# A conv stage rearranged: projection begun during the token tiles, products and low halves on VectorE, 36 taps ahead of attention

## The chip, the cores and the metric

The kernel runs on one core of a Trainium2 chip. The metric is the device time of one execution in microseconds. The five engines that matter are TensorE (matmuls and transposes, PE in the profile), VectorE (DVE), ScalarE (ACT), GpSimd (POOL) and SyncE (SP), whose queue issues almost all transfers.

## What is computed

One step of a hybrid decoder layer over 1024 prompt tokens and 8 x 8 sample tokens, padded to nine tiles of 128 tokens. The part that the change touches is the conv group of the input projection:

```python
xn = rmsnorm(h, g_mix)
z = xn @ w_in
q, k, v, og, lr, cv = jnp.split(z, SPLITS, axis=-1)
...
a, gate = jnp.split(cv, 2, axis=-1)
u = a * jax.nn.sigmoid(gate)
c, buf_new = causal_depthwise_conv(u, buf0, w_conv, b_conv)   # 31 taps per channel
c = jax.nn.silu(layernorm(c, g_conv_ln, b_conv_ln))
h = h + jnp.concatenate([o, c], axis=-1) @ w_out
```

`o` is the output of four heads of gated linear attention, computed in chunks. A top-2 mixture of 32 experts, a gated embedding and a last norm follow. All weights are fp32 and the matmuls of the projections run as three fp16 passes: each operand is split into a high half (its rounding to fp16) and a low half (the rest).

## The kernel before

The program is written by hand for each engine; semaphores order the engines, and within an engine the text order is the order of execution. Line numbers in this document are those of the kernel before, unless a row of the changed kernel shows others.

1. *Norm and transposes (0 to 36 us).* SP loads nine x tiles with two in flight (`load_x`, L492). ScalarE squares and takes the root (`norm_x`, L859 and L864), VectorE scales the tile by the gain (`norm_x`, L1199; two SBUF inputs), TensorE transposes it in eight pieces (`transpose_x`, L1668), ScalarE writes the high half (`evac_xT`, L869) and VectorE the low half (`evac_xT`, L1205; one input in PSUM).
2. *Conv projection (36 to 134 us).* For each of four channel groups c, TensorE computes part 0 (the gate) and then part 1 (a) for three blocks of 384 tokens, 24 matmuls a block and part (L1683), so 144 a group. ScalarE makes the high half of the group's weights w_cv[c] (`split_cv`, L878), GpSimd the low half (L687). ScalarE evacuates the gate with a sigmoid into `sg_sb` and a with a copy into `a_sb` (L914). GpSimd multiplies them into `u` (L702, L703). Beside this the 16 pieces of the token weights w_tok come in through two raw buffers, `side0` and `side1`: SP loads one when the low half of the piece before it in that buffer is done (`load_wt`, L505), ScalarE makes the high half (`split_wt`, L901), GpSimd the low half (L692). VectorE runs the depthwise taps of c = 0 and 1 once a group's `u` is there: tap 0 is a scale and a bias (L1235), each other one a multiply and add over 1024 tokens (L1238), and each waits for the one before. `REST = 9` of the 31 taps of a channel group are left for later, so 44 taps stand here. VectorE's next instruction after them is `log_gate(0)` (L1259).
3. *Attention (134 to 367 us).* TensorE projects tile n + 1 (`z`, L1691; `z_lr`, `z_qk`, `z_v`, `z_og`) among the attention steps of tile n: `turn` (L1735 to L1739), `scores` (L1746), `cumulate` (L1723, L1727; it wants `la` of VectorE), `outputs` (L1757 to L1761). Between its attention steps VectorE runs the taps that are left, `BESIDE` = 10 a tile, in groups of 3, 3 and 4. In a tile it does `qT_out` (L1275), 3 taps, `mask_scores` (L1279), `log_gate` (L1259), 3 taps, `state` (L1286), `decay_qk` (L1264, L1265), 4 taps, `gate` (L1270). GpSimd scales the state (L716, L718) and runs the taps of the sample tokens (L729, L733).
4. *Output stage, experts and the rest (367 to 1123 us).* VectorE first makes the low halves of w_out (L1316), whose raw buffers SP refills in turn; then come the conv's layer norm, the output projection, the router, the experts (L1907 to L1938), the embeddings (L1989, L1999). The change touches only names of semaphores here.

The order of the change's surroundings is set by these queues and by what each part waits for:

```python
pl.wait_ge(cv_sb, 6 * (c + 1))       # GpSimd's product: both parts of all three blocks
dve.wait_ge(u_rdy, 2 * (c + 1))      # VectorE's first tap of a group
pe.wait_ge(cv_sb, 6 * CC)            # TensorE before z_lr(0)
pe.wait_ge(wt_lo, 2 * KC)
```

## Time and profile before

| | us |
|---|---|
| three runs, median (lowest, highest) | 1126.66 (1126.3, 1128.25) |
| the profiled execution, its own time | 1125.14 |
| its span, first to last instruction | 1123.3 |
| TensorE busy | 1008.9 (90%) |
| VectorE busy | 721.1 (64%) |
| ScalarE busy | 473.6 (42%) |
| GpSimd busy | 295.3 (26%) |
| mean granted clock of TensorE | 0.946 |

The span is what the rows' times count from; the profiled execution's own time is 1.84 us longer. Busy shares are over the whole span, and a stage can have another limit than the mean shows. A row of the order of time reads: start, duration, engine, line, operation, output and inputs with their shapes, how many instructions are merged, and in brackets how long the engine stood idle before it and what released it. The granted clock is a share of TensorE's full speed: 1.0 is 2.4 GHz, 0.5 is 1.2 GHz.

### The profile page before, as it was taken

Reading aid. Unit: us, or ns where it says so; the run is one execution under the profiler, and the core shown is the slowest. Engines: PE = TensorE matmul, PEld = TensorE weight load, DVE = VectorE, ACT = ScalarE, POOL = GpSimd, SP = SyncE. Lnnn points to the kernel's source line nnn. Section 1 sums busy time; section 2 is a strip of 40 time slices with the busy share of each in tenths; the row PEclk is TensorE's granted clock in tenths of the full one; section 3 lists DMA queues with packets and bytes.
Section 4 is the critical chain, followed back from the end, with each engine's and each line's share of the span. In section 5 each row is a group of like instructions: output and inputs, shape, how many; then the busy total and the mean of one; then the engine's idle time right before and its main releaser. Section 6 shows DMA issues by size and latency. Waiting matters only on the chain.

```text
span 1123.3 us, 14888 instructions
## 1 busy us (share of the span) xinstructions
PE 1008.9 (90%) x4992; PEld 546.8 (49%) x4992; DVE 721.1 (64%) x830; ACT 473.6 (42%) x721; POOL 295.3 (26%) x267
## 2 busy tenths in 40 slices
PE   4899979999999978999429999999999999399996
PEld 3555535555555545555314555544444454144442
DVE  6259866667667596443586777776667675556552
ACT  7333122323222542322315655566555454434553
POOL 0567234656511522111011222222222223000000
PEclk9999989999999969999659999999999999699998
DMA  7443040000000602222647999999999977523321
GB/s 256 123 133 124 3 19 1 1 0 0 0 0 1 213 36 75 75 83 90 268 179 277 391 380 366 342 368 361 361 365 361 355 290 259 222 89 102 108 69 60
DMA packets 52234, 191.13 MB, mean 170 GB/s; under 512 B 19601, under 2 KB 20898, under 8 KB 37218
## 3 DMA queue, kind: packets, MB, share of 16 engines
q1 hardware_dynamic: 41250, 172.76, 43.6%
q0 software_dynamic: 10944, 17.85, 4.4%
q8 instruction: 23, 0.38, 0.1%
q14 instruction: 17, 0.14, 0.0%
HBM read 181.50 MB, written 31.09 MB: 189 GB/s over the span
## 4 chain that ended last, share of the span: by engine, by line
PE 63%; DVE 15%; DMA 11%; issue 4%; ACT 4%; POOL 2%; DVEq 1%; SPq 0%; POOLq 0%; ACTq 0%
PE psum L1691 12%; PE psum L1920 11%; PE psum L1999 8%; PE psum L1834 8%; DVE arena L1238 6%; DMA arena<-xn,ids 6%; PE psum L1938 6%; PE psum L1907 3%; PE psum L1989 2%; PE psum L1876 1%; PE psum L1758 1%; PE psum L1757 1%; DVE arena L1511 1%; DMA arena<-in_w_ple 1%; PE psum L1761 1%
## 5 line engine op out<-in xcount | busy, mean ns | idle before, releaser
L1920 PE MATMUL psum<-arena 128*128 128x512 f16 x888 | 201.8, 385 | 4.4 <-DVE arena L1515 4.4
L1238 DVE SCALAR_TENSOR_TENSOR arena<-arena,wc x120 | 185.9, 1549 | 17.3 <-DVE arena L1238 17.0
L1511 DVE TENSOR_TENSOR arena<-arena 128x1024 f16<-128x1024 f32 x148 | 174.2, 1217 | 2.6 <-ACT arena L1077 2.6
L1691 PE MATMUL psum<-arena 128*128 128x512 f16 (+1 forms) x864 | 153.1, 331 | 0.6 <-ACT arena L914 0.6
L1077 ACT ACTIVATE arena<-arena 128x1024 f16<-128x1024 f32 x148 | 147.1, 1047 | 0.0
L1920 PEld LDWEIGHTS psum<-arena 128*128 128x128 f16 x888 | 87.6, 99 | 104.6 <-DVE arena L1515 5.0
L1938 PE MATMUL psum<-arena 128*128 128x512 f32 x296 | 133.2, 593 | 1.2 <-DVE arena L1549 1.2
L1691 PEld LDWEIGHTS psum<-arena 128*128 (+1 forms) x864 | 68.2, 98 | 78.2 <-issue 8.7
L1683 PE MATMUL psum<-arena 128*128 128x384 f16 x576 | 96.3, 331 | 4.4 <-DVE arena L1205 2.4
L1999 PE MATMUL psum<-arena 128*128 128x512 f16 x432 | 96.8, 385 | 2.5 <-DVE arena L1620 2.5
L800 POOL DMA_INDIRECT yrows<-arena,idy x31 | 35.0, 1130 | 239.6 <-DVE arena L1549 232.0
L1834 PE MATMUL psum<-arena 128*128 128x512 f16 x432 | 97.0, 382 | 0.8 <-DVE arena L1366 0.8
L1938 PEld LDWEIGHTS psum<-arena 128*128 128x128 f32 x296 | 53.5, 190 | 54.6 <-issue 54.5
L1683 PEld LDWEIGHTS psum<-arena 128*128 128x128 f16 x576 | 56.8, 99 | 44.0 <-issue 5.2
L1907 PE MATMUL psum<-cst,arena 128*128 128x128 f32 x368 | 50.2, 281 | 27.4 <-DVE arena L1616 16.7
L1515 DVE TENSOR_TENSOR arena<-psum,arena 128x1024 f16<-128x1024 f32 x37 | 45.2, 1223 | 41.7 <-ACT arena L1081 41.7
L1999 PEld LDWEIGHTS psum<-arena 128*128 128x128 f16 x432 | 42.6, 99 | 53.6 <-issue 6.1
L1834 PEld LDWEIGHTS psum<-arena 128*128 128x128 f16 x432 | 42.6, 100 | 48.8 <-issue 1.1
L1085 ACT ACTIVATE arena<-psum 128x256 f32<-128x256 f32 x37 | 14.2, 384 | 121.8 <-PE psum L1920 121.8
L1907 PEld LDWEIGHTS psum<-cst,arena 128*128 128x128 f32 x368 | 43.4, 145 | 42.4 <-DVE arena L1616 17.5
L1539 DVE TENSOR_TENSOR arena<-arena,psum 128x256 f32<-128x256 f32 x37 | 15.6, 421 | 64.1 <-ACT arena L1085 64.1
L796 POOL DMA_INDIRECT arena<-xn,ids x34 | 35.8, 1054 | 78.7 <-DVE ids L1504 54.9
(239 smaller groups left out, 1267.2 us busy)
## 6 DMA issues: line engine op xcount, KB each, us to landing
arena<-in_w_gu SPq DMA_DIRECT2D x74, 1024.0 KB, 9.3
arena<-in_w_dn SPq DMA_DIRECT2D x37, 1024.0 KB, 7.2
arena<-yrows SPq DMA_DIRECT2D x18, 512.0 KB, 4.7
side<-in_w_tok SPq DMA_DIRECT2D x16, 388.0 KB, 3.3
arena<-in_x SPq DMA_DIRECT2D x9, 512.0 KB, 4.4
side<-in_x SPq DMA_DIRECT2D x9, 512.0 KB, 4.0
xn<-arena SPq DMA_DIRECT2D x9, 512.0 KB, 2.9
out_y<-arena SPq DMA_DIRECT2D x9, 512.0 KB, 3.0
```

The lines of the kernel that those rows point to most:

```text
L796: pl.indirect_dma_start(xg[s], None, a["xn2"], bass.IndirectOffsetOnAxis(rows_of, 0), bounds_check=TOK - 1, oob_is_err=False).then_inc(xg_ ...
L1077: act.activation(wsp[s][0][:, part], wgu[s][:, part], ACT.Copy).then_inc(ws_hi, 1)
L1238: dve.scalar_tensor_tensor(acc, src, w[:, k:k + 1], acc, ALU.mult, ALU.add).then_inc(conv, 1)
L1511: dve.tensor_tensor(wsp[s][1][:, part], wgu[s][:, part], wsp[s][0][:, part], ALU.subtract).then_inc(ws_lo, 1)
L1515: dve.tensor_tensor(xgT[s][1], psum[:, 0:2, :].rearrange("p a (b c) -> p (a b) c", c=P), xgT[s][0], ALU.subtract).then_inc(xgT_v, 1)
L1683: x = pe.matmul(psum[:, 3 * part + b, 0:BLK], wcv[c % 2][w][:, k, col:col + P], xnT[m][:, k, b * BLK:(b + 1) * BLK], start=k + w + m == 0, ...
L1691: x = pe.matmul(out, xnT[w][:, k, bass.ds(n * P, P)], wtok[m][:, k, col:col + width], start=k + w + m == 0, stop=k == KC - 1 and w == 1)
L1834: x = pe.matmul(psum[:, 2 * j + half, :], catT[j][w][:, k, :], wout[m][:, k, half * 512:(half + 1) * 512], start=k + w + m == 0, stop=k == ...
L1907: x = pe.transpose(psum[:, k // 4, (k % 4) * P:(k % 4 + 1) * P], src[:, k * P:(k + 1) * P], ident)
L1920: x = pe.matmul(psum[:, 2 + s, :], xgT[s][w][:, k, :], wsp[s][m][:, k, :], start=k + w + m == 0, stop=k == KC - 1 and w == 1)
L1938: x = pe.matmul(psum[:, 6 + half, :], hT[:, k, :], wdn[s][:, k, half * 512:(half + 1) * 512], start=k == 0, stop=k == FC - 1)
L1999: x = pe.matmul(psum[:, 2 + 4 * j + half, :], x3T[j][w][:, k, :], wgate[k][m][:, 0, half * 512:(half + 1) * 512], start=k + w + m == 0, st ...
```

## The change

It rearranges stages 1 and 2.

- SP: of the constant table only the identity is loaded ahead of the x tiles, the rest behind them; w_cv[0] goes between x2 and x3; w_cv[1] and the first two pieces of w_tok go ahead of the small loads; w_cv[2] and w_cv[3] go between pieces; the conv history follows all pieces.
- GpSimd makes both halves of w_cv[0] and nothing else of this stage.
- TensorE transposes tiles 0 to 3, then runs block (0, 0) and a quarter of (0, 1) with the transposes of tiles 4 to 8 between runs of 12 matmuls. It goes block by block, gate and then a, instead of part by part.
- ScalarE evacuates only the gate (sigmoid); `a_sb` is gone.
- VectorE multiplies a, read from PSUM, with the sigmoid (`glu_rows`), a block at a time, and makes the low halves of w_cv[1] to w_cv[3] and of w_tok. These steps stand after every fourth tap (`block_done`).
- `REST` is 13: 36 taps ahead of attention instead of 44, and 11 instead of 10 beside each tile of it, in groups of 3, 3 and 5.
- TensorE waits for all four groups' products (`u_rdy`) before `z_lr(0)`.

```diff
@@ sync
             load_x(0, 0)
             sp.dma_start(g1[:], a["g_mix"].to_broadcast([P, D])).then_inc(g1_in, 16)
-            sp.dma_start(cst[:], a["consts"]).then_inc(g1_in, 16)
+            sp.dma_start(cst[:, 0:P], a["consts"][:, 0:P]).then_inc(id_in, 16)
             load_x(1, 1)
+            load_x(2, 0)
+            sp.dma_start(wcv_raw, a["w_cv"][0]).then_inc(wcv_in, 16)
+            load_x(3, 1)
...
+            sp.dma_start(cst[:, P:CONST_W], a["consts"][:, P:CONST_W]).then_inc(g1_in, 16)
...
+            def load_cv(c):
+                sp.wait_ge(wcv_lo, c)
+                sp.dma_start(wcv_raw, a["w_cv"][c]).then_inc(wcv_in, 16)
+
+            load_cv(1)
+            load_wt(0, 0)
+            load_wt(0, 1)
...
+            for k in range(1, KC):
+                if k % NBLK == 0:
+                    load_cv(k // NBLK + 1)
+                for half in range(2):
+                    load_wt(k, half)
@@ gpsimd
-            split_cv(0)
-            for c in range(CC):
...
-                pl.tensor_tensor(u[:, c, HIST:UW], a_sb[:, 0:SEQ], sg_sb[:, 0:SEQ], ALU.mult).then_inc(u_rdy, 1)
...
+            pl.wait_ge(wcv_in, 16)
+            pl.tensor_copy(wcv[0][0], wcv_raw).then_inc(wcv_hi, 1)
+            pl.wait_ge(wcv_hi, 1)
+            pl.tensor_tensor(wcv[0][1], wcv_raw, wcv[0][0], ALU.subtract).then_inc(wcv_lo, 1)
@@ scalar
-                w_pieces(act, c, split_wt)
-                if c >= 1:
-                    act.wait_ge(u_rdy, 2 * c)
-                for part, (dst, fn) in enumerate([(sg_sb, ACT.Sigmoid), (a_sb, ACT.Copy)]):
-                    for b in range(NBLK):
-                        act.wait_ge(cv_ps, 6 * c + 3 * part + b + 1)
-                        act.activation(dst[:, b * BLK:(b + 1) * BLK], psum[:, 3 * part + b, 0:BLK], fn).then_inc(cv_sb, 1)
+                for b in range(NBLK):
+                    if c >= 1:
+                        act.wait_ge(u_rdy, 4 * (c - 1) + GLU[b])
+                    act.wait_ge(cv_ps, 6 * c + 2 * b + 1)
+                    act.activation(sg_sb[:, b * BLK:(b + 1) * BLK], psum[:, 2 * b, 0:BLK], ACT.Sigmoid).then_inc(cv_sb, 1)
+                    for k, half in pieces_beside(c, b):
+                        split_wt(k, half)
@@ vector
-            REST = 9
+            REST = 13
             BESIDE = (K + REST) // 4
-            with dve.Fori(0, CC // 2) as c:
-                taps(c, 0, K - REST, (K - REST) * c)
+
+            def glu_rows(c, b):
+
+                dve.wait_ge(cv_sb, NBLK * c + b + 1)
+                dve.wait_ge(cv_ps, 6 * c + 2 * b + 2)
+                end = min((b + 1) * BLK, SEQ)
+                n = end - b * BLK
+                dve.tensor_tensor(u[:, c, HIST + b * BLK:HIST + end], psum[:, 2 * b + 1, 0:n], sg_sb[:, b * BLK:end],
+                                  ALU.mult).then_inc(u_rdy, 1)
...
+            def split_wt(k, half):
+                dve.wait_ge(wt_hi, 2 * k + half + 1)
+                hi, lo = [w[:, k, half * TH:(half + 1) * TH] for w in wtok]
+                dve.tensor_tensor(lo, wt_raw[half], hi, ALU.subtract).then_inc(wt_lo, 1)
+
+            def block_done(c, b):
+
+                if b == 0 and c + 1 < CC:
+                    split_cv(c + 1)
+                glu_rows(c, b)
+                for k, half in pieces_beside(c, b):
+                    split_wt(k, half)
+
+            for b in range(NBLK):
+                block_done(0, b)
+            STEP = 4
+            for i in range(2 * (K - REST)):
+                taps(i // (K - REST), i % (K - REST), 1, i)
+                if i % STEP == STEP - 1:
+                    n = NBLK + i // STEP
+                    block_done(n // NBLK, n % NBLK)
@@ tensor
-            pe.wait_ge(g1_in, 32)
+            pe.wait_ge(id_in, 16)
...
+            for n in range(4):
+                transpose_x(n, n % 2)
+            pe.wait_ge(wcv_lo, 1)
+            pe.wait_ge(xnT_v, 3)
+            for part in range(2):
+                for q in range(2):
+                    x = conv_part(0, 0, part, range(4 * q, 4 * q + 4))
...
+                    n = 4 + 2 * part + q
+                    transpose_x(n, n % 2)
+            pe.wait_ge(xnT_v, 6)
...
+            pe.wait_ge(xnT_v, NT)
...
+                for b in range(NBLK):
+                    for part in range(2):
+                        if part:
+                            pe.wait_ge(u_rdy, 4 * (c - 1) + GLU[b])
+                        else:
+                            pe.wait_ge(cv_sb, NBLK * (c - 1) + b + 1)
+                        conv_part(c, b, part, range(KC)).then_inc(cv_ps, 1)
...
-            pe.wait_ge(cv_sb, 6 * CC)
+            pe.wait_ge(g1_in, 32)
+            pe.wait_ge(cv_sb, NBLK * CC)
+            pe.wait_ge(u_rdy, 4 * CC)
```

`pieces_beside(c, b)` gives the two halves of chunk 3c + b of w_tok, for the first eight of the twelve blocks.

Three places of the order. First TensorE from the start of the program to the token projection, before (L1668 are the transposes, eight a tile; L1683 the conv matmuls):

```order
L1668 MATMUL psum<-cst,arena 128x128 x8
L145 REGISTER_ALU
L145 COMPARE_AND_BRANCH
L1668 MATMUL psum<-cst,arena 128x128 x8
L1683 MATMUL psum<-arena 128x384 x576
L1691 MATMUL psum<-arena 128x16 x24
```

and now (L1688 the transposes, L1695 the conv matmuls):

```order
L1688 MATMUL psum<-cst,arena 128x128 x32
L1695 MATMUL psum<-arena 128x384 x12
L1688 MATMUL psum<-cst,arena 128x128 x8
L1695 MATMUL psum<-arena 128x384 x12
...
L1688 MATMUL psum<-cst,arena 128x128 x8
L1695 MATMUL psum<-arena 128x384 x516
L1735 MATMUL psum<-arena 128x16 x24
```

The conv matmuls begin behind four tiles' transposes instead of nine; the number of each kind is the same.

Then VectorE after the norms, before (L1235 a first tap, L1238 the others, in a loop over the two channel groups):

```order
L1240 MEMSET arena 128x4x64
L1245 UNCONDITIONAL_BRANCH
L1245 ISA
L1235 ISA x2
L1235 REGISTER_ALU
L1235 TENSOR_SCALAR arena<-arena,wc,cvec 128x1024
L1237 ISA
L1238 ISA
L1238 SCALAR_TENSOR_TENSOR arena<-arena,wc 128x1024
```

and now (L1244 the low half of a w_cv, L1236 and L1239 products, L1249 low halves of w_tok pieces, L1219 and L1222 taps):

```order
L1224 MEMSET arena 128x4x64
L1244 TENSOR_TENSOR arena<-arena 128x2048
L1236 TENSOR_TENSOR arena<-psum,arena 128x384
L1249 TENSOR_TENSOR arena<-side,arena 128x776 x2
...
L1219 TENSOR_SCALAR arena<-arena,wc,cvec 128x1024
L1222 SCALAR_TENSOR_TENSOR arena<-arena,wc 128x1024 x3
L1244 TENSOR_TENSOR arena<-arena 128x2048
L1236 TENSOR_TENSOR arena<-psum,arena 128x384
L1249 TENSOR_TENSOR arena<-side,arena 128x776 x2
L1222 SCALAR_TENSOR_TENSOR arena<-arena,wc 128x1024 x4
```

Products and low halves of the three blocks of c = 0 stand ahead of the first tap, those of the other nine behind each fourth tap, the last of them right ahead of `log_gate(0)`.

Last SP's queue from its second instruction on, before:

```order
L492 DMA arena<-in_x 128x1024
L495 DMA g<-in_g_mix 128x1024
L496 DMA cst<-in_consts 128x1416
L492 DMA arena<-in_x 128x1024
...
L492 DMA arena<-in_x 128x1024
L508 DMA arena<-in_w_cv 128x2048
```

and now:

```order
L483 DMA arena<-in_x 128x1024
L486 DMA g<-in_g_mix 128x1024
L487 DMA cst<-in_consts 128x128
L483 DMA arena<-in_x 128x1024 x2
L490 DMA arena<-in_w_cv 128x2048
L483 DMA arena<-in_x 128x1024
...
L496 DMA cst<-in_consts 128x1288
L504 DMA arena<-in_w_cv 128x2048
L500 DMA side<-in_w_tok 128x776 x2
```

The first w_cv is moved ahead of six x tiles and most of the constants behind all nine.

## Rows read from the trace of the kernel before

**Rows 1.** Chain of waits in order of time: start us, us, what.

```profile
67.35 4.19 DVE arena L1235
157.17 6.67 PE psum L1691 x24
```

**Rows 2.** TensorE in order of time, 0 to 165 us.

```profile
31.59 1.94 PE L1668 MATMUL psum<-cst,arena 128*128 128x128 f32 x8 [0.58 <-DVE arena L1205]
35.90 25.81 PE L1683 MATMUL psum<-arena 128*128 128x384 f16 x144 [2.38 <-DVE arena L1205]
...
87.31 46.96 PE L1683 MATMUL psum<-arena 128*128 128x384 f16 x288 [1.29 <-ACT arena L914]
134.86 5.96 PE L1691 MATMUL psum<-arena 128*128 128x16 f16 x48 [0.58 <-ACT arena L914]
...
141.91 5.35 PE L1691 MATMUL psum<-arena 128*128 128x512 f16 x24
155.00 1.22 PE L1723 MATMUL psum<-la,cst 128*128 128x256 f32 x2 [7.74 <-DVE la L1259]
...
157.10 6.74 PE L1691 MATMUL psum<-arena 128*128 128x512 f16 x24
```

**Rows 3.** VectorE and GpSimd in order of time, 90 to 155 us.

```profile
93.49 4.07 POOL L687 TENSOR_TENSOR arena<-arena 128x2048 f16<-128x2048 f32 x1
93.53 5.11 DVE L1238 SCALAR_TENSOR_TENSOR arena<-arena,wc  x1 [0.18 <-DVE arena L1238]
...
121.03 0.81 DVE L1235 TENSOR_SCALAR arena<-arena,wc,cvec  x1
...
153.33 1.28 DVE L1238 SCALAR_TENSOR_TENSOR arena<-arena,wc  x1 [0.18 <-DVE arena L1238]
```

**Rows 4.** Windows: stretch, its length, each engine's busy us, PEclk, DMA share, GB/s.

```profile
36.00:40.00 4.00, 4.00 (x13) 1.79 (x14) 0.45 (x3) 0.00 (x0) 0.00 (x0) 1.00 0.87 322
147.00:155.00 8.00, 0.26 (x2) 0.00 (x0) 7.05 (x7) 1.88 (x2) 0.00 (x0) 0.67 0.43 14
155.00:160.00 5.00, 5.00 (x17) 2.47 (x18) 0.76 (x2) 0.71 (x3) 1.93 (x2) 0.51 0.01 3
```

**Rows 5.** ScalarE, SP's queue and GpSimd in order of time: loads and who takes them.

```profile
9.63 1.06 ACT L859 ACTIVATE arena<-arena 128x1024 f32<-128x1024 f32 x1 [3.75 <-DMA arena<-in_x]
...
35.32 0.35 SPq L517 DMA_DIRECT2D arena<-in_w_cv  x1
...
40.08 1.91 ACT L878 ACTIVATE arena<-arena 128x2048 f16<-128x2048 f32 x1 [5.50 <-DMA arena<-in_w_cv]
...
46.10 3.27 POOL L692 TENSOR_TENSOR arena<-side,arena 128x776 f16<-128x776 f32 x2
...
51.23 0.85 ACT L901 ACTIVATE arena<-side 128x776 f32 x1 [7.75 <-DMA side<-in_w_tok]
```

**Rows 6.** Groups by line and shape, and one row of TensorE in the output stage.

```profile
L1316 DVE TENSOR_TENSOR arena<-arena 128x1024 f16<-128x1024 f32 x4 | 4.7, 1222 | 5.8 <-ACT arena L992 5.8
L1265 DVE TENSOR_TENSOR qk<-psum,E 128x256 f32<-128x256 f32 x9 | 3.7, 406 | 0.0
L771 POOL CAST arena<-arena 128x512 f16<-128x512 f32 x3 | 1.8, 611 | 24.1 <-ACT arena L1034 12.8 <-PE psum L1834 11.3
...
452.48 1.04 PE L1867 MATMUL psum<-cst,arena 128*128 128x128 f32 x8
```

**Rows 7.** One tile of attention in order of time, 208 to 234 us.

```profile
212.01 1.80 DVE L1238 SCALAR_TENSOR_TENSOR arena<-arena,wc  x1 [0.18 <-DVE arena L1238]
...
217.58 0.67 DVE L1275 COPY qkT<-psum 64x512 f32<-64x512 f32 x1
...
220.59 1.16 PE L1746 MATMUL psum<-qkT 64*128 64x128 f32 x8
...
225.00 0.42 DVE L1259 SCALAR_TENSOR_TENSOR la<-psum,absx 128x256 f32<-128x256 f32 x1 [1.70 <-ACT absx L931]
...
227.50 0.59 PE L1723 MATMUL psum<-la,cst 128*128 128x256 f32 x2
```

**Rows 8.** VectorE at the end of attention, 366 to 376 us.

```profile
373.15 2.36 DVE L1316 TENSOR_TENSOR arena<-arena 128x1024 f16<-128x1024 f32 x2 [0.81 <-ACT arena L992]
```

More of the change, by code:

```diff
@@ L470, in rows, with pieces_beside @@
             return t[bass.ds(n * P, P), :]
-        def w_pieces(eng, c, body):
-            first, last = [(0, 3), (3, 6), (6, KC), (KC, KC)][c]
-            if c == 0:
-                body(0, 0)
-                body(0, 1)
-                first = 1
-            if first < last:
-                with eng.Fori(first, last) as k:
-                    body(k, 0)
-                    body(k, 1)
+        def pieces_beside(c, b):
+            k = NBLK * c + b
+            return [(k, half) for half in range(2)] if k < KC else []
         block = ctx.enter_context(nc.Block())
@@ L893, in _ @@
             evac_xT(NT - 3, 0)
-            split_cv(0)
             evac_xT(NT - 2, 1)
@@ L1669, in transpose_x, with conv_part @@
                 x.then_inc(xT_ps, 1)
-            tiles(pe, transpose_x)
+            def conv_part(c, b, part, chunks):
+                col = P - P * part
+                for k in chunks:
+                    for w, m in PASSES:
+                        x = pe.matmul(psum[:, 2 * b + part, 0:BLK], wcv[c % 2][w][:, k, col:col + P],
+                                      xnT[m][:, k, b * BLK:(b + 1) * BLK], start=k + w + m == 0,
+                                      stop=k == KC - 1 and w == 1)
+                return x
@@ new lines, in _ @@
+            for n in range(4):
[5 more added lines that the diff above has]
+                    x = conv_part(0, 0, part, range(4 * q, 4 * q + 4))
+                    if q:
+                        x.then_inc(cv_ps, 1)
+                    n = 4 + 2 * part + q
+                    transpose_x(n, n % 2)
+            pe.wait_ge(xnT_v, 6)
+            for part in range(2):
+                for q in range(2):
+                    x = conv_part(0, 1, part, range(4 * q, 4 * q + 4))
+                    if q:
+                        x.then_inc(cv_ps, 1)
+                    elif part == 0:
+                        transpose_x(NT - 1, 0)
```

72 lines of the change are left out of this document (26 added, 46 removed).

## The prediction

> **What bounds the kernel now.** I read the chain of waits first, to see which engine carries the start of the program. At 67.35 us it passes to VectorE's depthwise taps [rows 1] and stays with them up to 155, though TensorE is full in most of this time. Then I read TensorE's own order of time [rows 2]. The conv projection runs from 35.90 to 134.3 us (the first 144 matmuls in 25.81 us, the last 288 in 46.96, 163 ns each), the token projections of tile 0 follow at 134.86, and then TensorE stands still from 147.26 to 155.00, waiting for `la`. The reader is to see why: `log_gate(0)` is queued on VectorE behind 44 taps, the last of which starts at 153.33 [rows 3]. So this stage has two limits that end at nearly the same place: TensorE's projection, and a tap chain that starts late.
>
> Why are the taps slow? The last ones take 1.28 us with 0.18 between, 1.46 in all, but the one that starts at 93.53 takes 5.11 us, beside a GpSimd subtraction of 4.07 us that began 0.04 us earlier [rows 3]. GpSimd's low halves and products hold the taps up through the whole stage.
>
> The windows show the price of the stall [rows 4]: the granted clock is 0.67 between 147 and 155 us and 0.51 (the 1.2 GHz level) from 155 to 160. The 24 matmuls of `z_og(0)` take 6.74 us there, where those of `z_v(0)` took 5.35 [rows 2]. Five microseconds at half clock are 2.4 us lost.
>
> **The front, worked out.** ScalarE can take x1 only at 9.63, since the broadcast gain and the whole constant table are queued ahead of it [rows 5]. Now only the identity of that table is ahead, and w_cv[0] goes behind x2. Six transfers up to and with w_cv (0.52 x 4 + 0.07 + 1.05 = 3.2 MB) at the 322 GB/s of the window at 36 us [rows 4] land 10 us after the first issue, and some 1 us is lost between the first two: 12 to 13 us, taken 13.0. GpSimd's copy: four times the 611 ns of 128x512 [rows 6], less the fixed parts, 2.3 us; its subtraction 4.07 [rows 3]. That gives low halves at 19.4. TensorE also wants three finished token tiles. VectorE's `norm_x(3)` is then in front of it and reads two SBUF tiles as a tap does. The tap of 5.11 us waited for the whole GpSimd subtraction and then ran about 1.1 [rows 3]; so I let `norm_x(3)` end at 20.6, then `evac_xT(1)`, `norm_x(4)`, `evac_xT(2)` at 1.22 + 1.45 + 1.22: the conv matmuls start at **24.0**. If the two engines did not exclude each other it would be 22.5.
>
> The Trainium skill ("SBUF — State Buffer", section "SBUF: two separate sides") states this as a rule: a VectorE instruction with two SBUF inputs and a GpSimd instruction that reads SBUF exclude each other for a whole instruction. It speaks against putting w_cv[0]'s low half on GpSimd inside the norms. No row of before shows GpSimd beside `norm_x`. By the rule the result is the sum below; without it the sum would be 1.5 us lower.
>
> From 24.0 TensorE works without a pause. Its first matmuls are slow: 13 in the 4 us from 36 [rows 4], 308 ns each against 163, though the granted clock reads 1.00 there. I keep this as 2 us. A group of eight transposes took 1.94 us here [rows 2], but 1.04 in the output stage, where TensorE is busy all the time [rows 6]; for the five remaining groups I take 1.04. So 144 matmuls (23.5 + 2) and five groups (5.2) end block (0,2) at **54.7**, and 432 more at 163 ns end the projection at **125.2**. Before it was 134.3.
>
> **VectorE.** Ahead of tile 8's transposes TensorE has 60 matmuls (9.8 + 2) and four other groups (4.2); with their own 1.04 they are done at 41.0; ScalarE and VectorE evacuate it by 43.4, small casts by 44.3. Then come split_cv(1), three products and six low halves of c = 0. I price them by size: a subtraction of 128x1024 takes 1222 ns and one of 128x256 with a PSUM operand 406 ns [rows 6], 1.04 to 1.06 ns a column. So 128x2048 is 2.3, 128x776 is 0.96, a product of 128x384 is 0.55, the third block's two products 0.62. These six pieces do not run back to back. The two raw buffers are refilled only when the low half is done: GpSimd's first piece ended near 47.7, and ScalarE got the next one at 51.23 [rows 5], 3.5 us; with ScalarE's 0.85 the round is 4.4 us plus VectorE's own 0.96. Two such rounds stand in the open, and the taps start at **60.1** instead of 67.35.
>
> From there VectorE is never idle, by this working. 36 taps: 34 x 1.46 + 2 x 0.99 = 51.6 (a channel's first tap took 0.81 alone [rows 3], plus 0.18 between). Two split_cv 4.6, nine blocks' products 6 x 0.55 + 3 x 0.62 = 5.2, ten low halves 9.6: 71.0; I add 0.4 for the semaphores of ScalarE in between, so VectorE is through at **131.5**. The round of 4.4 us hides under four taps (5.9 us). w_cv[2] and w_cv[3] take 4.8 us from issue at 35.32 to work at 40.08 [rows 5] and are issued a whole step before they are wanted. TensorE's part-1 matmuls wait for the product three blocks back: for block (2,0) that is done about 66 us and wanted at 82, for (3,2) done at 112 and wanted at 121. So the new waits of TensorE cost nothing, except the last: all products must be done before `z_lr(0)`, and the last product is queued behind all 36 taps. TensorE stands from 125.2 to 131.6.
>
> **The sum.** `z_lr(0)` starts at 131.6 where it started at 134.86: -3.3. It begins slow after 6.4 us of idling, +2.4 [rows 4], but `la` is now ready while `z_v(0)` still runs, so the stall of 7.74 us [rows 2] is gone, and with it the slow stretch behind it, -2.4. In attention each of eight tiles has 11 taps instead of 10, one more in the last group. In the tile shown [rows 7] `qT_out` starts at 217.58 and TensorE wants it at 220.59; VectorE waits 1.70 us for ScalarE before `la`, which TensorE wants 2.1 us later than it is ready. An added 1.46 fits in both: 0. At the last tile it does not quite. The scores themselves come later there, and only the 0.81 us that VectorE waited before the w_out low halves [rows 8] are left as a cushion; 1.46 less 0.81 makes those and the w_out transfers behind them 0.7 later. SP is moved too: w_tok and w_cv come between the small loads and the conv history, which is wanted only in attention, and the zero rows before attention come out near 100 us; 0.
>
> -3.3 + 2.4 - 7.7 - 2.4 + 0.7 = **-10.3 us**. The profiled execution took 1125.14 us (span 1123.3); with -10.3 it is 1114.8. The median of the runs is 1126.66, 1.5 higher, so I forecast **1116.4**. What comes after attention is unchanged in program and in its own waits.
>
> **The rivals.**
> *Better front and clock, 0.15.* w_cv[0] lands sooner or `norm_x` is not held up (-1.5 to -2), and TensorE's pause of 6.4 us does not cost the clock (-2.4). For it: the pause is shorter than the 7.74 that cost it. Against: the window 147 to 155 with 0.67 shows the fall well inside the pause. 1112 us.
> *Late front, 0.13.* x3 lands behind w_cv's 1 MB, GpSimd is itself held up by `norm_x`, and the interleaved transposes stay at 1.94 us. Five groups at +0.9 and 1 to 2 us of waiting make +5 or so: 1121 us.
> *The eleventh tap is on the path of every tile, 0.06.* This ends on the other side. Beside GpSimd's state products a tap takes 1.80 us [rows 7], 1.98 with its gap. Eight times 1.98 is 15.8, in place of the 0.7: -11.0 + 15.8 = +4.8, 1131.5 us. It decides from the point where VectorE's 1.70 us before `la` plus TensorE's 2.1 [rows 7] are used up. Against it: they are together twice the tap.
> *The refill round is not hidden, 0.03.* VectorE waits for a raw piece with four taps queued behind the wait. If each of the five tap steps with pieces waits its 4.4 us as c = 0 does, 22 us come on VectorE's chain: 1138 us. Against it: 5.9 us of taps in between.
> The forecast's own case has 0.63.
>
> **The numbers.** The range 1110.5 to 1122 holds the forecast's case and nearly all of the first two rivals; its lower end is the first rival's 1112 with the front another 1.5 us earlier, its upper end the late front with the full 1.46 in the tail. A measurement of this kernel tells 0.2% (2.3 us) from no change. Faster by more than that: 0.63 + 0.15 + 0.12 = 0.90; slower 0.08; within 0.02.
>
> **What would show it.** TensorE's first 128x384 matmul near 24 us, the last near 125; first tap near 60; taps all at 1.28 us before attention; last product and `z_lr(0)` near 131.5; no wait for `la` before `cumulate(0)`; granted clock low around 130; attention tiles as long as before. Wrong it would be by taps above 1.5 us with GpSimd idle, by low halves waiting for ScalarE between taps, by matmuls waiting on products inside the projection, or by attention tiles that are longer.

## The result, and the profile after

The changed kernel takes **1109.62 us** (median of 4 runs, 1108.4 to 1110.71), the one before 1126.49 beside it: ratio 0.9847, 95% interval 0.9829 to 0.9864. That is 16.9 us less. The forecast was 10.3 less (1116.4), and the result lies 0.9 us below the range's low end, so the prediction had the sign right and missed the size, since it had the order of the two longest chains wrong. The profiled execution of the changed kernel took 1110.71 us by its own time, with a span of 1108.5, where the one before took 1125.14 and 1123.3.

TensorE in order of time (start us, us, engine, line, what, count, and in brackets the idle time ahead and who ended it):

```profile
24.27 4.00 PE L1695 MATMUL psum<-arena 128*128 128x384 f16 x12 [0.79 <-DVE arena L1188]
28.06 1.64 PE L1688 MATMUL psum<-cst,arena 128*128 128x128 f32 x8
...
31.49 1.04 PE L1688 MATMUL psum<-cst,arena 128*128 128x128 f32 x8
...
40.83 84.01 PE L1695 MATMUL psum<-arena 128*128 128x384 f16 x516
125.72 5.94 PE L1735 MATMUL psum<-arena 128*128 128x16 f16 x48 [0.88 <-issue]
...
132.76 5.35 PE L1735 MATMUL psum<-arena 128*128 128x512 f16 x24
137.95 0.59 PE L1767 MATMUL psum<-la,cst 128*128 128x256 f32 x2
138.47 0.63 PE L1771 MATMUL psum<-cst,la 128*64 128x2 f32 x8
139.03 5.35 PE L1735 MATMUL psum<-arena 128*128 128x512 f16 x24
144.31 0.43 PE L1779 MATMUL psum<-cst,qk 128*64 128x128 f32 x2
```

The projection starts at 24.27 and ends at 124.84 (forecast 24.0 and 125.2). The 7.74 us in front of `cumulate(0)` are gone, and the 24 matmuls of `z_og(0)` take 5.35 us, not 6.74 [rows 2]. But `z_lr(0)` follows at once, at 125.72: the pause of 6.4 us that I expected ahead of it isn't there. Both numbers of VectorE's chain show why. VectorE in order of time, at its first steps and at its end:

```profile
60.02 0.81 DVE L1219 TENSOR_SCALAR arena<-arena,wc,cvec 128x1024 f32<-128x1024 f32 x1
...
69.12 5.24 DVE L1222 SCALAR_TENSOR_TENSOR arena<-arena,wc 128x1024 f32<-128x1024 f32 x4
74.28 0.55 DVE L1236 TENSOR_TENSOR arena<-psum,arena 128x384 f32<-128x384 f32 x1
74.74 1.83 DVE L1249 TENSOR_TENSOR arena<-side,arena 128x776 f16<-128x776 f32 x2
76.49 5.24 DVE L1222 SCALAR_TENSOR_TENSOR arena<-arena,wc 128x1024 f32<-128x1024 f32 x4
...
117.15 0.56 DVE L1236 TENSOR_TENSOR arena<-psum,arena 128x384 f32<-128x384 f32 x1 [0.46 <-PE psum L1695]
117.63 5.24 DVE L1222 SCALAR_TENSOR_TENSOR arena<-arena,wc 128x1024 f32<-128x1024 f32 x4
124.95 0.42 DVE L1236 TENSOR_TENSOR arena<-psum,arena 128x256 f32<-128x256 f32 x1 [2.09 <-PE psum L1695]
```

The taps start at 60.02 (forecast 60.1), but a step of four taps, a product and two low halves takes 76.49 - 69.12 = 7.37 us. By the prediction's prices it is 4 x 1.46 + 0.55 + 2 x 0.96 = 8.31. VectorE is at the last product 2.09 us before TensorE has finished the block for it. Now TensorE is the longer of the two chains, by 0.46 + 2.09 us.

The groups by line and shape tell the two kinds of tap apart: busy us and mean ns of one, then the idle time ahead of them. The 34 with shapes are those that stand written out ahead of attention, the 86 those in attention, whose column comes from a register:

```profile
L1222 DVE SCALAR_TENSOR_TENSOR arena<-arena,wc x86 | 123.1, 1431 | 11.2 <-DVE arena L1222 11.2
L1222 DVE SCALAR_TENSOR_TENSOR arena<-arena,wc 128x1024 f32<-128x1024 f32 x34 | 43.6, 1282 | 0.9
```

Where the columns come from registers, 11.2 us of idling lie ahead of 86 taps. Where they are constants, 0.9 us lie ahead of 34. All my taps were priced as the former [rows 3].

**Where the difference arises.** From TensorE's rows of the two kernels, start in us:

| first instruction of | before | after | difference |
|---|---|---|---|
| `z_lr(0)` | 134.86 | 125.72 | -9.1 |
| `q`/`k` transposes of tile 0 | 163.78 | 144.31 | -19.5 |
| the same of tile 8 (end of attention) | 366.91 | 348.90 | -18.0 |
| layer norm sums | 371.55 | 355.92 | -15.6 |
| dispatch, `upper16` matmul | 558.00 | 543.53 | -14.5 |
| end of the span | 1123.3 | 1108.5 | -14.8 |

The start gains more than forecast (19.5 against 11.0: the sum's -3.3 + 2.4 - 7.7 - 2.4), and 5 us are given back between 163 us and the dispatch. One part of that is in the tail of attention:

```profile
349.62 0.60 PE L1783 MATMUL psum<-cst,qk 128*64 128x128 f32 x4
353.92 2.07 PE L1790 MATMUL psum<-qkT 64*128 64x128 f32 x8 [3.70 <-DVE qkT L1295]
```

Before, TensorE waited 2.23 us for `qT_out` there and the eight matmuls took 1.16. Now it waits 3.70, one tap of 1.47 more, and they take 2.07. The other part is TensorE's clock. The windows (start:end, length, busy us of PE, PEld, DVE, ACT, POOL, then PEclk, DMA share, GB/s) of the changed kernel:

```profile
121.00:145.00 24.00, 22.77 (x138) 11.34 (x137) 3.56 (x7) 7.89 (x14) 5.60 (x8) 1.00 0.59 24
162.50:165.50 3.00, 3.00 (x12) 2.17 (x13) 0.32 (x2) 0.60 (x1) 0.00 (x0) 0.50 0.00 0
353.50:360.50 7.00, 6.58 (x16) 4.32 (x17) 3.37 (x4) 6.57 (x7) 6.42 (x33) 0.51 0.45 157
```

Around `z_lr(0)` the clock stays full, so the +2.4 of the sum isn't there. But at 162.5 it is at its lower level of 1.2 GHz for 3.4 us while TensorE is 100% busy with the small fp32 matmuls of `outputs`. Summed over half-microsecond windows, each window's length times what its granted clock lacks to 1.0, such a **dip** comes to 1.71 us. There are four in attention, 51 us or two tiles apart (162, 213.5, 264.5, 316). The kernel before had three there (231.5, 282.5, 334). Without the dips attention is 203.1 - 5.1 = 198.0 us long before and 204.6 - 6.8 = 197.8 after. Around the end of the pause of 3.70 us, at 353.92, the clock is low for 7 us, 3.4 lost.

### The profile page after: what moved, and what is told of

Same layout as the page of the kernel before. It is cut to its first block, busy times and chain, and to the rows that moved or that the text cites. A ratio compares the mean times of both kernels' runs of the same rounds, so it can differ in the third digit from the quotient of the medians.

```text
span 1108.5 us, 14663 instructions
## 1 busy us (share of the span) xinstructions
PE 1005.0 (91%) x4992; PEld 547.1 (49%) x4992; DVE 727.9 (66%) x865; ACT 467.3 (42%) x708; POOL 244.6 (22%) x241
## 4 chain that ended last, share of the span: by engine, by line
PE 76%; DMA 10%; DVE 7%; ACT 3%; issue 3%; POOL 1%; SPq 0%; DVEq 0%; POOLq 0%; ACTq 0%
PE psum L1735 13%; PE psum L1966 12%; PE psum L1695 9%; PE psum L2045 9%; PE psum L1880 8%; PE psum L1984 7%; DMA arena<-xn,ids 7%; PE psum L1953 3%; PE psum L2035 3%; PE psum L1922 1%; PE psum L1802 1%; PE psum L1801 1%; PE psum L1805 1%; DMA arena<-in_x 1%; DMA arena<-in_w_ple 1%
## 5 line engine op out<-in xcount | busy, mean ns | idle before, releaser
L1222 DVE SCALAR_TENSOR_TENSOR arena<-arena,wc (+1 forms) x120 | 166.7, 1389 | 12.2 <-DVE arena L1222 11.2
L1695 PE MATMUL psum<-arena 128*128 128x384 f16 x576 | 96.5, 330 | 0.8 <-DVE arena L1188 0.8
L1695 PEld LDWEIGHTS psum<-arena 128*128 128x128 f16 x576 | 56.8, 99 | 38.8 <-issue 2.9
L1559 DVE TENSOR_TENSOR arena<-arena,psum 128x256 f32<-128x256 f32 x37 | 15.6, 421 | 63.8 <-ACT arena L1068 63.8
L1064 ACT ACTIVATE arena<-psum 128x1024 f16<-128x1024 f32 x37 | 37.9, 1023 | 39.0 <-PE psum L1953 39.0
```

The source lines that it names most:

```text
L1064: act.activation(xgT[s][0], psum[:, 0:2, :].rearrange("p a (b c) -> p (a b) c", c=P), ACT.Copy).then_inc(xgT_a, 1)
L1222: dve.scalar_tensor_tensor(acc, src, w[:, k:k + 1], acc, ALU.mult, ALU.add).then_inc(conv, 1)
L1695: x = pe.matmul(psum[:, 2 * b + part, 0:BLK], wcv[c % 2][w][:, k, col:col + P], xnT[m][:, k, b * BLK:(b + 1) * BLK], start=k + w + m == 0, ...
```

## The experiments

All of them compute the whole result; e9 to e11 do some matmuls twice. "Lost" is the sum described above, over the half-microsecond windows of the profiled execution up to 601 us. It counts a window whether TensorE works in it or not, so it is more than the time that the lower clock cost: in the changed kernel 23.9 of the 46.1 us fall between 527.5 and 575.5, where TensorE is busy for only 14.07 of 48 us. A difference of 1.7 between two kernels is one dip. Times are medians with their range; `z_lr(0)`, transposes, dispatch and span are of one profiled execution each.

| kernel | time us | runs | `z_lr(0)` | tile 0 transposes | dispatch | lost | span |
|---|---|---|---|---|---|---|---|
| before | 1126.49 | 4 | 134.86 | 163.78 | 558.00 | 46.1 | 1123.3 |
| after | 1109.62 | 4 | 125.72 | 144.31 | 543.53 | 46.1 | 1108.5 |
| e8 (after again) | 1110.17 (1107.28-1111.04) | 5 | 124.89 | 143.48 | 542.67 | 46.1 | 1105.1 |
| e1 register columns | 1105.24 (1102.95-1107.66) | 4 | 125.11 | 143.70 | 540.72 | 41.0 | 1101.1 |
| e2 before, unrolled | 1120.11 (1118.42-1126.02) | 10 | 135.51 | 160.73 | 551.59 | 41.0 | 1117.6 |
| e3 8 taps behind | 1106.67 (1105.68-1107.81) | 4 | 124.53 | 143.13 | 540.72 | 41.0 | 1104.2 |
| e4 late projection | 1117.76 (1111.94-1118.96) | 6 | 134.47 | 153.07 | 550.89 | 44.4 | 1114.6 |
| e5 44 taps ahead | 1115.72 (1114.37-1117.08) | 4 | 133.39 | 154.24 | 547.36 | 44.4 | 1112.6 |
| e6 e3 + norm free | 1101.71 (1098.94-1104.96) | 6 | 123.72 | 142.32 | 539.11 | 41.0 | 1100.0 |
| e7 GpSimd pieces | 1108.06 (1104.56-1109.74) | 4 | 125.73 | 144.33 | 544.64 | 44.4 | 1107.4 |
| e9 shift 1.5 | 1109.94 (1108.62-1111.79) | 4 | 126.45 | 145.04 | 542.29 | 44.4 | 1107.2 |
| e10 shift 3.4 | 1110.78 (1108.36-1113.18) | 4 | 128.39 | 146.99 | 546.02 | 46.1 | 1110.8 |
| e11 shift 6.8 | 1115.29 (1113.18-1117.21) | 5 | 130.99 | 149.58 | 544.68 | 41.0 | 1112.5 |

The kernel before took 1126.87 beside e1 to e4, 1127.13 beside e5 to e8 and 1128.02 beside e9 to e11. As ratios to it, with 95% intervals, where a difference has to be clear of noise:

| kernel | ratio | interval |
|---|---|---|
| after | 0.9847 | 0.9829 to 0.9864 |
| e8 (after again) | 0.9848 | 0.9817 to 0.9880 |
| e1 | 0.9824 | 0.9794 to 0.9855 |
| e3 | 0.9832 | 0.9803 to 0.9862 |
| e4 | 0.9912 | 0.9882 to 0.9942 |
| e5 | 0.9900 | 0.9863 to 0.9938 |
| e6 | 0.9776 | 0.9744 to 0.9808 |
| e7 | 0.9820 | 0.9780 to 0.9859 |
| e9 | 0.9846 | 0.9802 to 0.9890 |
| e10 | 0.9844 | 0.9796 to 0.9891 |
| e11 | 0.9893 | 0.9859 to 0.9928 |

So e4 and e6 differ from the changed kernel, and e5 from e3 (just), beyond their intervals. The intervals of e1, e3, e7 and e9 to e11 meet the changed kernel's, and what their medians say of it is a hint. Rows of like programs vary too: the nine profiled executions with the changed kernel's front start their first conv matmul between 23.39 and 24.70 us.

**e1. The taps priced as I priced them: columns from registers.** The two theories are that the cheaper constant-column taps made the difference to the forecast, or something else did.

```diff
-            for i in range(2 * (K - REST)):
-                taps(i // (K - REST), i % (K - REST), 1, i)
+                    with dve.Fori(s // 2, s // 2 + 2) as hh:
+                        for q in range(2):
+                            i = 2 * hh + q
+                            k = i - c * (K - REST)
+                            dve.wait_ge(conv, i)
...
```

> The changed kernel with 28 of the 36 taps ahead of attention in small loops, so that their columns come out of a register as in the kernel before; order and work are the same. Theory A (the taps run back to back in the changed kernel, 5.24 us for four instead of 5.86, because their addresses are constants): the 0.18 us gap comes back for these 28, some 4 us, and the branches of seven loops add 1 to 3. Of this 2.1 us are hidden by the slack before the last product. z_lr(0) starts 3 to 5 us later than 125.7; if TensorE's pause is then long enough for its clock to fall, 2 more are lost: 1113 to 1117 us. Theory B (the taps are quicker only because GpSimd is silent): no change, 1109.6 us, four taps still in 5.24 us.

VectorE of e1:

```profile
68.29 1.28 DVE L1271 SCALAR_TENSOR_TENSOR arena<-arena,wc 128x1024 f32<-128x1024 f32 x1
69.74 1.28 DVE L1271 SCALAR_TENSOR_TENSOR arena<-arena,wc 128x1024 f32<-128x1024 f32 x1 [0.18 <-DVE arena L1271]
...
72.64 1.28 DVE L1271 SCALAR_TENSOR_TENSOR arena<-arena,wc 128x1024 f32<-128x1024 f32 x1 [0.17 <-DVE arena L1271]
73.84 0.55 DVE L1236 TENSOR_TENSOR arena<-psum,arena 128x384 f32<-128x384 f32 x1
...
124.35 0.42 DVE L1236 TENSOR_TENSOR arena<-psum,arena 128x256 f32<-128x256 f32 x1
```

The gap of 0.18 us comes back with the registers, and four taps take 73.84 - 68.29 = 5.55 us instead of 5.16: the step between two taps is 1.45, between the last tap and the product 1.20. So over half of the mis-sizing of a step (0.39 of 0.68 us) is the register, and the rest is that I put the gap behind the last tap of each group too and let no instruction overlap the next (their records overlap by 0.08). The step from the second to the third tap, across the loop's turn, is no longer than the others, so the branches that I priced at 1 to 3 us cost nothing that shows. The time went against what I expected (1113 to 1117): seven such groups lengthen the chain by 7 x 0.39 = 2.7 us, TensorE's slack takes nearly all of it (the last product starts with no wait, at 124.35), and the median is 4.4 us below the changed kernel's, not above it. By the ratios that lead isn't clear of noise. The trace has one difference to show for it: 5.1 us less are lost to the clock, and the first dip in attention comes at 236. That this is the cause isn't shown.

**e2. Only the taps of the kernel before written out.**

```diff
-            with dve.Fori(0, CC // 2) as c:
+            for c in range(CC // 2):
                 taps(c, 0, K - REST, (K - REST) * c)
```

> The kernel before, with its 44 taps ahead of attention written out instead of in a loop over two channel groups; nothing else. Theory A (constant addresses let taps start back to back): up to 0.15 us a tap, 6 us in all, so la is ready 6 us sooner, the 7.7 us stall before cumulate(0) shrinks to under 2 and the clock does not fall behind it: 1117 to 1120 us. Theory B (only GpSimd's silence quickens taps): 1126 us.

It is faster by 0.5% (ratio 0.9949, 0.993 to 0.9968), but `cumulate(0)` starts only 3.2 us sooner (151.76 for 155.00), not 6, and TensorE still waits 3.85 us there, where I expected under 2; the clock falls there again. 5.1 us less are lost to the clock. Beside GpSimd the taps gain little from their form, 2.5 us each here:

```profile
77.52 25.24 DVE L1238 SCALAR_TENSOR_TENSOR arena<-arena,wc 128x1024 f32<-128x1024 f32 x10
```

Writing the taps out alone gives the smaller part of the change's gain.

**e3. 8 of the 44 taps behind the last product.**

```diff
-            REST = 13
+            REST = 9
...
-                if i % STEP == STEP - 1:
+                if i % STEP == STEP - 1 and NBLK + i // STEP < NBLK * CC:
```

> The changed kernel with REST 9 again: 44 taps ahead of attention, eight of them behind the last product and ahead of la, and 10 instead of 11 beside each tile. Theory A: these eight end 10.5 us after the products, at 136, and la cannot start before 136.8 anyway, so they are free; at the end of attention qT_out comes 1.5 us sooner and TensorE's pause before the last scores is 2.2 us instead of 3.7, which spares its clock: 1107 to 1108.5 us. Theory B: la gets late by what its own queue costs, and the tail's gain is eaten: 1109.6 us or more.

VectorE of e3:

```profile
124.24 10.99 DVE L1222 SCALAR_TENSOR_TENSOR arena<-arena,wc 128x1024 f32<-128x1024 f32 x8
135.62 0.42 DVE L1279 SCALAR_TENSOR_TENSOR la<-psum,absx 128x256 f32<-128x256 f32 x1 [0.40 <-ACT absx L914]
```

Eight taps fit between the last product and `la` with 0.4 us to spare. They are the hole of 11.3 us that the changed kernel leaves there. Each tile of attention is back at 10 taps; the last scores come sooner (a pause of 2.24 us for 3.70) and their clock dip is one instead of two. The median, 1106.67, is 0.3 below the 1107 to 1108.5 of Theory A, but its lead over the changed kernel isn't clear of noise.

**e4. The projection starts when all nine tiles are transposed.** This undoes one part.

```diff
-            for n in range(4):
+            for n in range(NT):
                 transpose_x(n, n % 2)
             pe.wait_ge(wcv_lo, 1)
-            pe.wait_ge(xnT_v, 3)
-            for part in range(2):
-                for q in range(2):
...
             pe.wait_ge(xnT_v, NT)
```

> The changed kernel, but all nine tiles are transposed before the first conv matmul, as in the kernel before; block by block order and everything on the other engines stay. Theory A (TensorE is the bound up to z_lr(0)): the projection starts near 36 instead of 24.3 and ends 9 us later, 1118 to 1120 us. Theory B (VectorE's chain is the bound and TensorE has slack): 1 to 3 us later only, 1111 to 1113 us.

The first conv matmul moves from 24.27 to 38.16 and `z_lr(0)` from 125.72 to 134.47, 8.8 us; the transposes now stand ahead of it instead of inside. The time follows, +7.6 to +8.1, just under Theory A's range. TensorE's chain is what bounds this stage, and the early projection is nearly half of the gain. The rest of it shows in e4 against the kernel before: `z_lr(0)` starts at nearly the same time (134.47 for 134.86), and tile 0's transposes 10.7 us sooner (153.07 for 163.78), with no wait for `la` and no slow stretch behind it. No run tells how much of that comes from the silent GpSimd, how much from the form of the taps and how much from eight taps fewer.

**e5. All 44 taps ahead of the last product, five between two products.** This makes VectorE's chain the longer one on purpose.

```diff
-            REST = 13
+            REST = 9
...
-            STEP = 4
+            STEP = 5
...
-                if i % STEP == STEP - 1:
+                if i % STEP == STEP - 1 or i == 2 * (K - REST) - 1:
```

> The changed kernel with REST 9, as e3, but a product after every fifth tap, so that all 44 taps stand ahead of the last product and z_lr(0) waits for them. Theory A (the wait of z_lr(0) for the last product is what VectorE's chain costs; the chain had 2 to 3 us to spare): eight taps of 1.31 us on the chain are 10.5 us, less the slack 7 to 8 us on TensorE's pause, which is then 8 to 9 us long, so its clock falls for one or two stretches of 1.7 us lost each: 8 to 11 us over e3's 1106.7, 1114.5 to 1118 us. Theory B (TensorE's path sets the end and taps are free): 1107 us.

TensorE and the windows of e5:

```profile
133.39 8.21 PE L1735 MATMUL psum<-arena 128*128 128x16 f16 x48 [8.87 <-issue]
```

```profile
124.00:128.00 4.00, 0.52 (x4) 0.10 (x1) 3.93 (x5) 0.00 (x0) 0.00 (x0) 1.00 0.00 0
128.00:139.00 11.00, 5.61 (x37) 2.48 (x38) 5.07 (x6) 0.18 (x1) 1.75 (x3) 0.53 0.60 30
```

Here is the case that the prediction described, with a longer pause: TensorE stands for 8.87 us behind the product, the clock falls inside the pause, and `z_lr(0)` takes 8.21 us, not 5.94. The mechanism and its price (2.4 us forecast, 8.21 - 5.94 = 2.3 here) were right; whether a pause of 6.4 us costs the same no run shows. What was wrong is that 36 taps would reach it.

**e6. e3, with the low half of w_cv[0] on VectorE behind the second transposed tile.**

```diff
-            pl.tensor_tensor(wcv[0][1], wcv_raw, wcv[0][0], ALU.subtract).then_inc(wcv_lo, 1)
...
-            with dve.Fori(1, (NT - 1) // 2) as i:
...
+            for n in range(2, NT - 1):
+                norm_x(n, n % 2)
+                evac_xT(n - 2, n % 2)
+                if n == 3:
+                    dve.wait_ge(wcv_hi, 1)
+                    dve.tensor_tensor(wcv[0][1], wcv_raw, wcv[0][0], ALU.subtract).then_inc(wcv_lo, 1)
```

> e3 (44 taps, the last eight behind the last product), and the low half of w_cv[0] is made by VectorE behind evac_xT(1) instead of by GpSimd; VectorE's norms are written out for this. Theory A (GpSimd's subtraction of 4.07 us kept norm_x(3) waiting, 4.8 us where it needs 1.28): norm_x(3) takes 1.28, the subtraction costs VectorE 2.2, and the projection starts 1 to 1.5 us sooner; all of it reaches the end: 1105 to 1106 us. Theory B (norm_x(3) is slow for another reason): no row changes but the subtraction's, and the start is 2 us later.

VectorE of the changed kernel and of e6 at `norm_x(3)`; in the former GpSimd's subtraction of 4.06 us runs from 15.12:

```profile
15.67 4.59 DVE L1182 SCALAR_TENSOR_TENSOR arena<-arena,rst,g 128x1024 f32<-128x1024 f32 x1 [0.15 <-DVE rst L1178]
```

```profile
15.50 1.28 DVE L1179 SCALAR_TENSOR_TENSOR arena<-arena,rst,g 128x1024 f32<-128x1024 f32 x1
16.70 1.22 DVE L1185 TENSOR_TENSOR arena<-psum,arena 128x1024 f16<-128x1024 f32 x1
17.83 2.28 DVE L1195 TENSOR_TENSOR arena<-arena 128x2048 f16<-128x2048 f32 x1
```

The norm takes 1.28 us instead of 4.59, and VectorE does the subtraction in 2.28. The conv matmuls start at 22.79, sooner than in any kernel with the other front (23.39 to 24.70), and `z_lr(0)` at 123.72, 0.8 sooner than in e3. It is the fastest of all, 1101.71 us, and its interval doesn't meet that of the changed kernel beside it. It just meets e3's, and 1101.71 is more than 3 us below the 1105 to 1106 that I expected: 0.8 us of the lead over e3 are there at `z_lr(0)` and 1.6 at the dispatch; where the rest comes from isn't shown.

**e7. The sixteen `w_tok` low halves back on GpSimd.**

```diff
+            for k in range(KC):
+                for half in range(2):
+                    pl.wait_ge(wt_hi, 2 * k + half + 1)
+                    hi, lo = [w[:, k, half * TH:(half + 1) * TH] for w in wtok]
+                    pl.tensor_tensor(lo, wt_raw[half], hi, ALU.subtract).then_inc(wt_lo, 1)
...
-                for k, half in pieces_beside(c, b):
-                    split_wt(k, half)
```

> The changed kernel with the 16 low halves of w_tok back on GpSimd; products and w_cv stay on VectorE. Theory A (the two engines exclude each other, so that moving these halves to VectorE is a gain of little more than nothing on VectorE's chain): ten pieces leave the chain, -9 us, and each keeps a tap waiting by about 1.2 us, +12 us; VectorE ends 1 to 4 us later than in the changed kernel, partly in its slack: 1109 to 1113 us. Theory B (no hindrance): VectorE has 9 us more to spare, TensorE is the bound, 1108 us, and all taps take 1.28.

VectorE of e7:

```profile
66.61 8.74 DVE L1228 SCALAR_TENSOR_TENSOR arena<-arena,wc 128x1024 f32<-128x1024 f32 x4
75.27 0.54 DVE L1242 TENSOR_TENSOR arena<-psum,arena 128x384 f32<-128x384 f32 x1
```

Four taps take 8.74 us, not 5.24, beside GpSimd's pieces of 128x776. VectorE is rid of about 1.8 us of its own per step and pays 3.5 there (2.6 in the third such step, of 7.84 us): the move to VectorE is a gain where both run together. As a whole it is even: the last product waits 0.16 us for TensorE where it waited 2.09, so the loss used up the slack, and `z_lr(0)` starts at 125.73, as in the changed kernel. The median, 1108.06, is 0.9 below Theory A's range and at Theory B's value; the rows speak for A.

**e8. The changed kernel once more, in the session of e5 to e7.**

> The changed kernel once more, beside the others on one chip. Theory A (its time moves by a few times 1.7 us, by how many stretches of half clock fall into attention and its end, four and two in the first profile): 1105 to 1111 us, and e3 1.5 us below it. Theory B (time is fixed by the program): 1109.6 us within 0.2%.

Its dips in attention are at 161.5, 212.5, 263.5 and 315, where the first profile had them at 162, 213.5, 264.5 and 316, and the same 46.1 us are lost. The changed kernel's mean granted clock was 0.945 or 0.946 in all nine of its executions. But a program doesn't fix the clock in general: of e10's four executions two have 0.946 and take 1113.0 and 1113.2 us, the other two have 0.950 and take 1108.4 and 1108.5. From 542.67 on the same code took 2.5 us less than in the first profile (562.4 against 565.0), with no dip to show for it: that much of a single span stays unexplained.

**e9 to e11. TensorE kept busy 1.5, 3.4 and 6.8 us longer ahead of `z_lr(0)`.** The question is whether the dips explain why e1's median is lower.

```diff
                             pe.wait_ge(cv_sb, NBLK * (c - 1) + b + 1)
+                        for _ in range(9 if (c, b, part) == (CC - 1, NBLK - 1, 1) else 0):
+                            pe.matmul(psum[:, 2 * b + part, 0:BLK], wcv[c % 2][0][:, 0, 0:P],
+                                      xnT[0][:, 0, b * BLK:(b + 1) * BLK], start=True, stop=True)
                         conv_part(c, b, part, range(KC)).then_inc(cv_ps, 1)
```

> The changed kernel with 9 matmuls of the last projection block done once more for nothing ahead of it (overwritten; the result is complete): TensorE stays busy and z_lr(0) starts 9 x 163 ns = 1.5 us later, nothing else differs. Theory A (what is left of the difference between like kernels comes from where short half-clock stretches fall in attention, and these move with the program's time): z_lr(0) near 126.8, but the time doesn't follow by 1.5; the stretches between turn(0) and 600 us fall elsewhere or change in number, each worth 1.7 us, so the time lies between 1107 and 1113. Theory B (the stretches belong to places in the program): same number of them at places 1.5 us later, time 1109.6 + 1.5 = 1111.1 within 1.

> The same with 21 matmuls: 3.4 us. Theory A: z_lr(0) near 128.7; number and places of the half-clock stretches change, time between 1108 and 1115, not in line with 1.5 and 6.8. Theory B: 1113.0 within 1, stretches 3.4 us later than in the changed kernel, the same number.

> The same with 42 matmuls: 6.8 us. Theory A: z_lr(0) near 132.1; time between 1110 and 1119, with the number of half-clock stretches accounting for what differs from 6.8. Theory B: 1116.5 within 1. This is also the start of z_lr(0) that the prediction named (131.6) with no pause ahead of it: if the prediction's other terms were right (no clock loss) the time from here would be 1116.4 - 2.4 = 1114.0.

The same instruction, the state product of tile 0, in the changed kernel and in e9, and e9's window (columns as above):

```profile
163.06 1.97 PE L1805 MATMUL psum<-v,qk 128*64 128x128 f32 x8
```

```profile
163.50 1.09 PE L1808 MATMUL psum<-v,qk 128*64 128x128 f32 x8
```

```profile
162.50:165.50 3.00, 3.00 (x19) 1.99 (x19) 0.76 (x3) 0.60 (x1) 0.00 (x0) 1.00 0.00 0
```

Against e8, `z_lr(0)` is 1.56, 3.50 and 6.10 us later, and the dispatch -0.38, +3.35 and +2.01. The differences are -1.9, -0.2 and -4.1, and the lost time says -1.7, 0.0 and -5.1. So e9 is without one dip and e11 without three (one each in attention, in its tail and behind it), and e10 has the changed kernel's, 2.5 us later. Theory A holds for the traces: a delay of 6.1 us cost 2.0 up to the dispatch. e10's profile is of one of its two slower executions, and the other two, 4.7 us faster, have none. In the medians it shows less: +0.0, +0.9 and +5.4 against 1109.9, the mean of the changed kernel's two medians. For e11 that is nearly the whole delay, as Theory B had it; its profiled span is 7.4 us above e8's but 4.0 above the first profile's. What the parts behind the dispatch add isn't settled: they took 562.4 to 567.8 us in these five profiles, with the same code. The clock explains part of it at most: near 950 us four of them have 21 us at half clock and e11 has 24. So a difference of 3 us between two single spans shows nothing here. At the dispatch e1 is 2.8 us ahead of the changed kernel's first profile (540.72 for 543.53) and 2.0 ahead of its second (542.67), with 5.1 less lost. At `z_lr(0)` it was 0.6 ahead of the first and 0.2 behind the second. So 2.2 us of its lead arise between, where the dips are: the clock can explain that much, and not all that it takes is on the path.

## Why the prediction was wrong, point by point

**The bound: right.** TensorE's projection and VectorE's chain were to end close together. e4 and e5 show both sides: delay TensorE's start by 14 us and `z_lr(0)` goes 8.8 later; put e3's last eight taps ahead of the last product and it goes 8.9 later than in e3.

**The front: right.** Conv matmuls at 24.27 (forecast 24.0), block by block to 124.84 (125.2). `norm_x(3)` was held up as the sum had it, ending at 20.26 (20.6): GpSimd's subtraction ran from 15.12 to 19.18, and the norm that began beside it took 4.59 us, 1.28 without it in e6. The Trainium skill ("SBUF — State Buffer", section "SBUF: two separate sides") says that such a pair excludes one another for a whole instruction. The rows of the changed kernel, of e6 and of e7 agree with it: 4.59 us for the norm beside the subtraction and 1.28 without, four taps in 8.74 us beside GpSimd's pieces and in 5.24 without. The sum's 1.5 us for a front without the exclusion has no run of its own: e6 starts 0.7 us sooner than e3, but there VectorE has 2.28 us of work more, and like fronts start up to 1.3 us apart. The interleaved transposes fell to 1.04 us from their second group on, as taken.

**The start of the taps: right** (60.02 for 60.1; with the same program ahead of it 58.69 in e8 and 61.02 in e3, so that the 0.1 is luck), and so was the claim that the ring of raw buffers is covered from there on.

**The chain of 71.0 us: wrong, and this is the step that failed.** To the last tap the sum had 70.8 (71.0 + 0.4, less the last product's 0.62); it measured 117.63 + 5.24 - 60.02 = 62.9 us, 0.46 of it waiting for TensorE. I took 1.46 us a tap from a row of a loop whose columns come from registers [rows 3], while the change writes the taps out with constants. Four taps to the product take 5.16, not 5.84: nine groups make 6.1 us, and the other 2 us are overlaps of about 0.08 at each of the other instructions and the 0.4 added for semaphores. The order of instructions showed both forms, loop and written out, and I didn't ask what the form costs. e1 gives the answer: 0.39 of the 0.68 us is the register.

**What followed from it.** With VectorE through before TensorE, `z_lr(0)` starts at the projection's end plus 0.88: -9.1 where the sum had -3.3. The +2.4 of clock isn't incurred. Both were one mistake. The rival *better front and clock* had the second half of it, for a shorter pause; no rival said that there would be no pause. e5 shows that the rest of the reasoning holds when the pause is made. These two terms were 5.8 and 2.4 us too dear, 8.2 together, and the sum is only 4.5 off in the spans because attention, the tail and the part up to the dispatch cost 4 us that it didn't have. That they made up for half of the mistake is luck.

**The stall and the slow stretch behind it: right.** From `z_lr(0)` to tile 0's transposes the kernel before took 28.92 us and this one 18.59, so 10.3 less; the sum had 7.7 + 2.4 = 10.1.

**Attention 0: right in its waits, not in its time.** The eleventh tap hides: without the dips 198.0 and 197.8 us. The dips were not in the sum. The changed kernel has four where the one before has three; the fourth is 1.7 us, which makes attention 1.5 longer. By e9 to e11 their number changes with shifts of a few us, so that this term came out as it did is chance.

**The tail of +0.7: too small.** I charged the tap to the low halves only, with a cushion of 0.81. It lies in front of the scores as well, TensorE waits 3.70 us instead of 2.23, and then starts at half clock. The layer norm sums are 2.4 us late against the start of tile 8's transposes (-15.6 against -18.0), of which 1.47 is the tap and 0.9 the scores' slower matmuls. I had noted that the scores come later and priced nothing for it.

**The sum, again, with what was measured:** -9.14 - 10.33 + 1.46 (attention) + 2.38 (scores) + 1.16 (up to the dispatch) - 0.33 (behind it) = -14.8 in the spans of the two profiles; the medians are 16.9 apart. By their own times the two executions are 14.4 apart; the one before lies 1.4 below its median and the one after 1.1 above, which makes up the 16.9.

## What to carry to other kernels

Before a duration is multiplied, look at the form of the instruction it comes from: a loop's row holds gaps that written-out code doesn't have, and the last of a group has none. Where two chains are forecast to end within a few per cent of each other (here 131.5 against 125.2 after 70 us), the order of the two is a case of its own and wants a chance, with its knock-on effects (here the clock) attached to it. And when a chain turns out to have slack, put work into the hole behind it, not ahead of it: eight taps behind the last product (e3) cost nothing and took a tap out of every tile.

## What the runs showed of the hardware

- Dependent VectorE instructions with constant columns step by 1.32 us (four in 5.24) at 1.28 us of work; with columns from registers by 1.46, with 0.18 us of idling on record (e1, where the taps stand in small loops, and the loop of the kernel before).
- TensorE's granted clock falls to its lower level for about 3.4 us (1.71 lost) in the middle of attention, with TensorE 100% busy, and there it begins among the small fp32 matmuls of `outputs`. Most come 51 us apart, two tiles; e3, e4 and e7 have some of twice the length, and then the next comes 102 us after. How many there are (one in e2, three in e1 and e6, four in the changed kernel) changes with shifts of 1 to 6 us and no other edit (e9 to e11), and the mean clock can differ between executions of one program (0.946 and 0.950 in e10, 4.7 us apart). What sets them off isn't shown.
- A pause of TensorE of 3.70 us ahead of the last scores came with 7 us at half clock (3.4 lost), in the changed kernel, e7, e8, e9 and e10. One of 2.23 to 3.44 at the same place came with 3.5 to 4 us (1.7 lost), in the kernel before, e1 to e5 and e11. Behind the one of 1.56 in e6 the clock stayed full at first; its next low stretch begins at 371.5, 23 us on.
- VectorE's taps beside GpSimd's subtractions: 8.74 us for four against 5.24 (e7), and in e2 2.5 us each.
